# Attention sublayer: the output product done in two halves of the tokens, the first of them inside the attention steps

## The reference, cut to what matters

```
score = where(causal, sum_h relu(q_idx @ k_idx) * w_idx, -inf)      # per query token
sel   = top_k(score, 128)                                           # keys kept
logits= where(valid, q_lat @ c_sel * dh**-0.5, -inf);  p = softmax(logits)
o     = (p @ c_sel) @ w_uv                                          # 512 x 1024
x     = x + o.reshape(512, 1024) @ w_out                            # the output product
```

## Time and profile before

| | us |
|---|---|
| median of 3 runs (lowest, highest) | 2018.43 (2018.05, 2019.6) |
| the profiled execution itself | 2018.26 |
| its span, first to last instruction | 2016.4 |
| TensorE busy | 1980.2 |
| VectorE, ScalarE, GpSimd busy | 1346.0, 844.5, 249.7 |
| attention steps, turn_probs(0) to the first output matmul | 1554.35 to 1613.14 |
| output product | 1613.14 to 1656.80 |

### The profile page before, as it was taken

How to read it: one execution, slowest core, us unless ns; L and a number is a source line. 1 busy time by engine, 2 the same in 40 slices (tenths; PEclk the granted TensorE clock), 3 DMA queues, 4 the chain that set the end, 5 groups by cost and what they waited for, 6 DMA issues and landing times.

```text
span 2016.4 us, 23083 instructions
## 1 busy us (share of the span) xinstructions
PE 1980.2 (98%) x9030; PEld 1618.4 (80%) x9030; DVE 1346.0 (67%) x1673; ACT 844.5 (42%) x1151; POOL 249.7 (12%) x183
## 2 busy tenths in 40 slices
PE   8999999999999999999999999999998899999997
PEld 7788888877877888888888888888875688888886
DVE  7999944443534447999843899983458658999732
ACT  5555632132222224554631555562266535555520
POOL 0000012010010141000021000002224650000031
PEclk9999999999999999999999999999999999999998
DMA  4233123312212232242131333222231013322221
GB/s 168 84 122 129 58 102 112 113 64 100 84 68 85 82 105 84 84 147 104 58 115 64 119 141 110 84 87 100 81 105 42 1 63 142 109 84 98 100 93 65
DMA packets 69719, 189.45 MB, mean 94 GB/s; under 512 B 4016, under 2 KB 12208, under 8 KB 64496
## 3 DMA queue, kind: packets, MB, share of 16 engines
q1 hardware_dynamic: 69376, 187.25, 26.5%
q0 software_dynamic: 240, 0.79, 0.1%
HBM read 185.92 MB, written 2.10 MB: 93 GB/s over the span
## 4 chain that ended last, share of the span: by engine, by line
PE 87%; DVE 6%; issue 3%; ACT 2%; POOL 1%; SPq 0%; DMA 0%; POOLq 0%; DVEq 0%; ACTq 0%
PE bank L1804 13%; PE bank L1806 13%; PE bank L1805 13%; PE bank L1812 12%; PE bank L1814 12%; PE bank L1813 12%; PE bank L1818 2%; PE bank L1820 2%; PE bank L1819 2%; PE bank L2021 2%; PE bank L1911 2%; DVE part_lo L1182 1%; PE bank L2011 1%; PE bank L2130 1%; POOL dsa_temp L712 1%
## 5 line engine op out<-in xcount | busy, mean ns | idle before, releaser
L741 ACT ACTIVATE part_hi<-quad_w 128x1024 fp32r<-128x1024 f32 x280 | 293.2, 1064 | 279.5 <-PE bank L1814 199.8
L1182 DVE TENSOR_TENSOR part_lo<-quad_w,part_hi 128x1024 fp32r<-128x1024 f32 x280 | 330.0, 1217 | 25.7 <-ACT part_hi L741 25.3
L1804 PE MATMUL bank<-gated_hi,out_hi 128*128 128x512 f32 x704 | 274.8, 390 | 0.0
L1806 PE MATMUL bank<-gated_hi,out_lo 128*128 128x512 f32 x704 | 274.1, 389 | 0.0
L1805 PE MATMUL bank<-gated_lo,out_hi 128*128 128x512 f32 x704 | 274.1, 389 | 0.0
L1812 PE MATMUL bank<-part_hi,s_hi 128*128 128x512 f32 x640 | 252.6, 395 | 2.4 <-DVE part_lo L1182 2.4
L1814 PE MATMUL bank<-part_hi,s_lo 128*128 128x512 f32 x640 | 249.6, 390 | 0.0
L1813 PE MATMUL bank<-part_lo,s_hi 128*128 128x512 f32 x640 | 249.2, 389 | 0.0
L1812 PE MATMUL bank<-part_hi,xn_hi 128*128 128x512 f32 x608 | 238.8, 393 | 4.7 <-DVE part_lo L1182 4.7
L1814 PE MATMUL bank<-part_hi,xn_lo 128*128 128x512 f32 x608 | 237.9, 391 | 0.0
L1813 PE MATMUL bank<-part_lo,xn_hi 128*128 128x512 f32 x608 | 237.7, 391 | 0.0
(11 more groups left out here) (207 smaller groups left out, 3385.8 us busy)
## 6 DMA issues: line engine op xcount, KB each, us to landing
quad_w<-w_ffn_in SPq DMA_DIRECT2D x80, 1024.0 KB, 7.3
out_raw<-w_ffn_out SPq DMA_DIRECT2D x64, 704.0 KB, 4.0
w_raw<-w_ret_in SPq DMA_DIRECT2D x24, 1024.0 KB, 4.8
rest_raw<-w_ffn_in SPq DMA_DIRECT2D x32, 256.0 KB, 5.8
w_raw<-w_ret_out SPq DMA_DIRECT2D x8, 1024.0 KB, 4.8
w_raw<-w_dsa SPq DMA_DIRECT2D x8, 1024.0 KB, 4.8
x_res<-x_in SPq DMA_DIRECT2D x8, 256.0 KB, 6.3
out<-x_res SPq DMA_DIRECT2D x8, 256.0 KB, 2.2
```

The source lines that it names most:

```text
L741: nc.scalar.activation(in_four(part_hi[part_slot(h)]), source, copy).then_inc(part_hi_made, 1)
L1182: nc.vector.tensor_tensor(in_four(part_lo[part_slot(h)]), source, in_four(part_hi[part_slot(h)]).bitcast(FP32), ALU.subtract)\
L1804: mm(to, w_hi_of[:, at:at + width], hi, start=start, stop=False)
L1806: return mm(to, w_lo_of[:, at:at + width], hi, start=False, stop=stop)
```

## The change

The output product is done in two halves of 256 tokens. The first (blocks 0 and 1, "early") is done one tile a step at the head of steps 18 to 25, into bank 7, and VectorE adds each tile to `x_res` at the end of the same step of its list. The second ("late") follows the steps, into banks 0 and 1; its first two tiles begin with the heads 0 to 3. All four weight units are split before: units 8 and 9 get places of their own (where `xn_hi` and `xn_lo` lie), 10 and 11 go to the slots of `w_hi` and `w_lo`. ScalarE makes their hi at steps 2, 6 and 10 (before: unit 9 at step 8, 10 and 11 in the output product), GpSimd their lo: unit 9 before its step 8, unit 10 before step 12, unit 11 before step 16. Two rounds of the choice move from before step 0 into the steps, three steps have two rounds, and `result_hi` and `result_lo` come one step earlier. In the output phase the first four `stream_lo` wait until tile 3 is done.

```diff
--- before.py
+++ after.py
+    dsa_out_parts = [(at(f"dsa_out_hi{n}", x_at + (1 + n) * CHUNKS * chunk, UNIT, FP32R),
+                      at(f"dsa_out_lo{n}", x_at + (1 + n) * CHUNKS * chunk + 4 * UNIT, UNIT, FP32R))
+                     for n in range(2)]
...
-    ROUND_STEPS = (8, 10, 11, 13, 14, 16, 17, 18, 19, 20)
-    EARLY_ROUNDS = TOP_K // 8 - len(ROUND_STEPS)
-
-    POOL_SPLITS = (DSA_UNITS - DSA_OUT_UNITS - 2, DSA_UNITS - DSA_OUT_UNITS + 2)
+    ROUNDS_AT = {8: 1, 10: 1, 12: 1, 14: 1, 16: 1, 17: 1, 18: 2, 19: 2, 20: 2}
+    EARLY_ROUNDS = TOP_K // 8 - sum(ROUNDS_AT.values())
+    CHOICE_STEP = max(ROUNDS_AT) + 1
+    EARLY_OUT = 18
+    POOL_SPLITS = (DSA_UNITS - DSA_OUT_UNITS - 2, DSA_UNITS)
...
     def results_bank(q):
-        return bank[5 + q % 3]
+        return bank[5 + q % 2]
+    def early_out():
+        return bank[7][:, :HALF_SEQ]
+    def late_out(d):
+        return bank[d % 2][:, :HALF_SEQ]
...
                 split_unit(u0 + POOL_SPLITS[0] + 2)
+                split_unit(u0 + POOL_SPLITS[0] + 3)
                 for i in range(VECTOR_STEPS, len(STEPS)):
+                    if i == 2 * HEADS - 4:
+                        split_unit(u0 + POOL_SPLITS[0] + 4)
+                    elif i == 2 * HEADS:
+                        split_unit(u0 + POOL_SPLITS[0] + 5)
                     _, _, probs, _, _, at = step_bufs(i)
                     pool.wait_ge(inverted, i + 1)
                     nc.gpsimd.tensor_scalar(probs, probs, row_inv[:, at], None, ALU.mult)\
                         .then_inc(pool_probs_done, 1)
-                split_unit(u0 + POOL_SPLITS[0] + 3)
...
-            if n >= 2 and SUBLAYERS[stage_of(u)] != "ffn":
+            if SUBLAYERS[stage_of(u)] == "dsa" and n >= DSA_UNITS - DSA_OUT_UNITS:
+                act.wait_ge(unit_done, u - 3)
+            elif n >= 2 and SUBLAYERS[stage_of(u)] != "ffn":
                 act.wait_ge(unit_done, u - 1 + 2 * pair)
...
                 for i in range(len(STEPS)):
-                    if i == HEADS:
-                        split_unit(u0 + 9)
+                    if i in (2, 6, 10):
+                        split_unit(u0 + DSA_UNITS - DSA_OUT_UNITS + 1 + i // 4)
                     copy_probs_t(i)
                     if i + 2 < len(STEPS):
                         exps(i + 2)
-                    if i % 4 == 1 and i > 4:
+                    if i % 4 == 0 and i >= 4:
                         result_hi(i // 4 - 1)
                 result_hi(len(STEPS) // 4 - 1)
+                act.wait_ge(unit_done, u0 + DSA_UNITS - DSA_OUT_UNITS + 1)
                 for d in range(CHUNKS):
-                    if d % 2 == 1 and d // 2 + 2 < DSA_OUT_UNITS:
-                        split_unit(u0 + DSA_UNITS - DSA_OUT_UNITS + 2 + d // 2)
...
+                def early_update(d):
+                    dve.wait_ge(early_out_done, d + 1)
+                    to = cols(x_res, d)[:, :HALF_SEQ]
+                    nc.vector.tensor_tensor(to, early_out(), to, ALU.add).then_inc(early_updated, 1)
+                def late_update(d):
+                    to = cols(x_res, d)[:, HALF_SEQ:]
+                    nc.vector.tensor_tensor(to, late_out(d), to, ALU.add).then_inc(x_updated, 1)
                 for i in range(len(STEPS)):
                     invert(i)
                     if i + 2 < len(STEPS):
                         minimum(i + 2)
-                    if i in ROUND_STEPS:
+                    if i % 4 == 1 and i > 4:
+                        result_lo(i // 4 - 1)
+                    for n in range(ROUNDS_AT[i] if i in ROUNDS_AT else 0):
+                        if n > 0:
+                            mark_8(last_block)
                         find_8(last_block)
-                    elif i == ROUND_STEPS[-1] + 1:
+                    if i == CHOICE_STEP:
                         choice_to_bias(last_block)
-                    if i % 4 == 2 and i > 4:
-                        result_lo(i // 4 - 1)
+                    if 0 <= i - EARLY_OUT < CHUNKS:
+                        early_update(i - EARLY_OUT)
...
-                    update(s, d, 4 + d % 2, 1.0)
-                    if d % 2 == 1 and d // 2 + 2 < DSA_OUT_UNITS:
-                        split_unit(u + 2)
-                    stream_lo(s + 1, d)
+                    late_update(d)
+                    if d == 3:
+                        for e in range(4):
+                            stream_lo(s + 1, e)
+                    elif d > 3:
+                        stream_lo(s + 1, d)
...
+                def out_products(to, d, tokens, ks):
+                    u = u0 + DSA_UNITS - DSA_OUT_UNITS + d // 2
+                    pe.wait_ge(w_lo_made, u + 1)
+                    for k in ks:
+                        done = product(to, None, (d % 2 * HEADS + k) * P, cols(o_hi, k)[:, tokens],
+                                       cols(o_lo, k)[:, tokens], k == 0, k == HEADS - 1,
+                                       of=unit_bufs(u)[1:])
+                    return done
+                early, late = slice(0, HALF_SEQ), slice(HALF_SEQ, SEQ)
                 for i in range(len(STEPS)):
+                    d = i - EARLY_OUT
+                    if 0 <= d < CHUNKS:
+                        if d == 0:
+                            pe.wait_ge(o_lo_made, 4)
+                        else:
+                            pe.wait_ge(early_updated, d)
+                        out_products(early_out(), d, early, range(HEADS)).then_inc(early_out_done, 1)
                     turn_probs(i)
...
+                pe.wait_ge(o_lo_made, 7)
+                for d in range(2):
+                    out_products(late_out(d), d, late, range(HEADS // 2))
+                pe.wait_ge(o_lo_made, 8)
                 for d in range(CHUNKS):
...
+                    ks = range(HEADS // 2, HEADS) if d < 2 else range(HEADS)
+                    out_products(late_out(d), d, late, ks).then_inc(unit_done if d % 2 else half_done, 1)
```

More of the change, by code:

```diff
@@ L409, in unit_bufs @@
             return out_raw[n], out_hi[n], out_lo[n]
+        n = u - FIRST_UNIT[s] - (DSA_UNITS - DSA_OUT_UNITS)
+        if SUBLAYERS[s] == "dsa" and 0 <= n < 2:
+            return (w_raw[u % 2],) + dsa_out_parts[n]
         return w_raw[u % 2], w_hi[u % 2], w_lo[u % 2]
@@ L673, in split_unit @@
                     pool.wait_ge(w_lo_made, u)
-                    nc.gpsimd.tensor_tensor(w_lo[u % 2][:, :], w_raw[u % 2][:, :],
-                                            w_hi[u % 2][:, :].bitcast(FP32), ALU.subtract)\
+                    raw, hi, lo = unit_bufs(u)
+                    nc.gpsimd.tensor_tensor(lo[:, :], raw[:, :], hi[:, :].bitcast(FP32), ALU.subtract)\
                         .then_inc(w_lo_made, 1)
@@ L1744, in invert @@
                     nc.vector.reciprocal(row_inv[:, at], row_sum[:, at]).then_inc(inverted, 1)
-                    if i - 1 in ROUND_STEPS:
+                    if i - 1 in ROUNDS_AT:
                         mark_8(last_block)
@@ L2193, in results @@
                     pe.wait_ge(probs_t_copied, i + 1)
-                    if i % 4 == 0 and i >= 12:
-                        pe.wait_ge(o_lo_made, i // 4 - 2)
+                    if i % 4 == 0 and i >= 8:
+                        pe.wait_ge(o_lo_made, i // 4 - 1)
                     for j in range(b + 1):
@@ L2209, in _ @@
                 results(len(STEPS) - 1)
+                pe.wait_ge(o_lo_made, 7)
+                for d in range(2):
+                    out_products(late_out(d), d, late, range(HEADS // 2))
+                pe.wait_ge(o_lo_made, 8)
                 for d in range(CHUNKS):
-                    u = u0 + DSA_UNITS - DSA_OUT_UNITS + d // 2
-                    if d % 2 == 0:
-                        pe.wait_ge(w_lo_made, u + 1)
                     if d >= 2:
                         pe.wait_ge(x_updated, CHUNKS * s + d - 1)
-                    for k in range(HEADS):
-                        if d == 0:
-                            pe.wait_ge(o_lo_made, len(STEPS) // 4 - 1 + k // 4)
-                        done = product(bank[4 + d % 2][:, :], u % 2, (d % 2 * HEADS + k) * P,
-                                       cols(o_hi, k), cols(o_lo, k), k == 0, k == HEADS - 1)
-                    done.then_inc(unit_done if d % 2 else half_done, 1)
+                    ks = range(HEADS // 2, HEADS) if d < 2 else range(HEADS)
+                    out_products(late_out(d), d, late, ks).then_inc(unit_done if d % 2 else half_done, 1)
         final = ("norm", len(SUBLAYERS))
```

3 lines of the change are left out of this document (2 added, 1 removed).

## The result

The changed kernel takes 2033.57 us (median of 4 runs, 2033.13 to 2034.17) against 2018.24 of the kernel before: a ratio of 1.0073, interval 1.0059 to 1.0087. It is slower by 15.3 us, where 2033.0 was forecast. The profiled execution has a span of 2032.1 us, 15.7 more than before.

The account below looks back on a forecast made before the run. TensorE, busy 98% of the span, was taken as the bound, with some 13 us of waits to win. Terms: 9.8 + 22.0 - 0.4 - 20.6 + 3.0 + 1.0 = +14.8 on 2018.26, forecast 2033.0 us, range 2023 to 2039.

Parts of the forecast that it names:

- TensorE was to be idle for 6 us at turn_probs(4): Step 4: TensorE idle 6 us while VectorE's scaling takes about 4 us beside GpSimd's pass over unit 9.
- Start of the steps: Ahead of step 0: two rounds fewer, then ScalarE's table load is what comes late; -2.8 us.
- Units 9 and 10 through step 8: Steps 0 to 8: GpSimd's unit 9 pass stops VectorE's scaling, +4.9 us; ScalarE's unit 10 pass costs +1.5.
- GpSimd's passes ahead of scalings 12 and 16: Steps 12 and 16: units 10 and 11 each cost 4.60 less 0.85 idle time, 3.75 us; +7.4 after catching up.
- What goes between step 8 and the first early tile: Steps 8 to 18: 0.69 us waiting ahead of turn_probs(18) and unit 9's 0.5 behind step 8 go; -1.2 us.
- Clock: Half clock behind TensorE's idle stretches: one shrinks ahead of step 0, three new ones come; +1.0 us, ends -1 and +4.
- Early half: Steps 18 to 25: 192 matmuls add 23.0 us, product changes 0.5, idle time of 1.53 goes; net +22.0.
- Steps 26 to 31, late half and what lies behind it: After the early tiles: steps 26 to 31 -0.4 us, late half -20.6, late first weight part ahead of next sublayer +3.0.
- The extra cost of the two halves: Output product: 256 columns take more than half of 512, so both halves cost TensorE 2.4 us more than one product.
- A: Rival, steps 4 to 7: VectorE is not stopped by GpSimd's pass; 3.9 us less, 2029.2; chance 0.13.
- B: Rival, steps 12 and 16: GpSimd's passes half hidden; 3.7 to 5.5 less, 1 less at end, 2027.5; chance 0.13.
- C: Rival, whole change: faster if every split fits in its engine's idle time; -4.0 us, 2014.3; chance 0.11.

Follow-up runs that it names:

- experiment 6: On the changed kernel, units 9 to 11 split late: ScalarE behind steps 17, 19, 21, GpSimd ahead of scalings 19, 21, 23; 2017.28 us, ratio 0.9993.
- experiment 2: On the changed kernel, GpSimd's pass over unit 9's low part covers only 16 of 2048 columns; 2030.89 us, ratio 1.0060.
- Experiment 4: On the changed kernel, GpSimd's pass over unit 9 issued as 8 instructions of 256 columns, nothing left out; 2031.79 us, ratio 1.0064.
- experiment 3: On the changed kernel, GpSimd's passes over units 10 and 11 cover only 16 of 2048 columns each; 2023.77 us, ratio 1.0027.
- experiment 9: On the kernel before, only VectorE's rounds placed as in the changed kernel, no early tiles, no unit moved; 2019.71 us, ratio 1.0006.
- experiment 8: On the changed kernel, the edits of experiment 6 and experiment 7 together, nothing left out; 2013.79 us, ratio 0.9976.
- experiment 1: On the kernel before, the output product behind the steps done with each tile in two halves of 256 columns; 2021.34 us, ratio 1.0016.
- experiment 7: On the changed kernel, late half's VectorE work reordered: next sublayer's rest one tile earlier, stream_lo spread over tiles 3 to 7; 2030.60 us, ratio 1.0059.
- experiment 5: On the changed kernel, units 10 and 11 split later: ScalarE behind steps 19, 21, GpSimd ahead of scalings 21, 23; 2024.81 us, ratio 1.0028.
- experiment 10: Changed kernel, GpSimd's three passes ahead of scalings 19, 21, 23, ScalarE's unit 11 at step 21, units 9, 10 unmoved; 2020.51 us, ratio 1.0008.

## Why the prediction was right, and which terms were not

The forecast's mechanism held at the places that it named: the scaling of VectorE at 3.88 us once, waits of 4 us at turn_probs(12) and (16), no wait from the first early tile to turn_probs(26), a late part_lo. One sign was off: TensorE was to be idle for 6 us at turn_probs(4), and it was for 4.01, with another 0.89 just ahead, where it waited for ScalarE's copy. By terms:

- Start of the steps: -2.8 forecast, -2.95 measured. Right. Of the 4.05 us of idle time 1.28 are left, behind ScalarE's table load, which makes -2.77; the rest lies ahead of it.
- Units 9 and 10 through step 8: +4.9 and +1.5 forecast, 6.4 together. 6.21 measured (experiment 6 against the changed kernel), 4.05 of it GpSimd's pass and 2.16 ScalarE's two. Right. (Half clock is in it: from turn_probs(4) to (8) there are 6.25 us, and 5.79 in experiment 2, where the clock stays at 1.00.) The Trainium skill ("SBUF — State Buffer", on the port pair that VectorE and GpSimd share) has the two exclude each other for the whole instruction. Experiment 4 agrees with that: pieces of 0.70 us delay a scaling by at most 0.5, where the whole pass delayed it by 3.6.
- GpSimd's passes ahead of scalings 12 and 16: +7.4. The two waits shrank by 7.2 in experiment 3. Right.
- What goes between step 8 and the first early tile: -1.2 forecast. Experiment 6, with no pass left there, takes 16.96 us from turn_probs(8) to that tile for 18.40 before: -1.4. Right.
- Clock: +1.0 forecast, within ends of -1 and +4. This is the term that was too small. The granted clock went to 0.50 behind each of the three long stops, for 3.5 to 5.8 us of its work, and TensorE was the bound in part of each. At the first early tile experiment 3 has 9.9 less, and the waits make 7.2 of it: 2.7 us. With the half clock behind the late half, where sum_over_features comes 12.43 us after the sublayer's start for 10.88, 1.5 more come outside the steps. That is 4.2 us, against which stands what before lost behind its one stop: 0.9 by turn_probs(4) and 0.7 by turn_probs(8), as experiment 9 shows. So +1.0 should have been +3.3 to +3.5.
- Early half: +22.0 forecast, +20.6 measured (37.87 less 17.25). This term was too large. A tile takes 2.96 us, so 23.7 for the 23.5 that I had, but the steps' own work beside it takes 14.2 and not 15.72. I read this as follows, without a run made for it: busy time of matmuls counts each one's end, which lies under the next one's start where TensorE doesn't stop. What goes with the waits is therefore 3.1, and not the 1.53 that the windows show as idle.
- Steps 26 to 31, late half and what lies behind it: -0.4, -20.6 and +3.0, -18.0 together. Measured: 39.99 for 58.02, -18.0. One by one: steps 26 to 31 take 13.72 for 14.36, -0.6. The late tiles take 23.11 in experiment 8, where nothing stops them, -20.6. The changed kernel's 26.27 make the stop worth 3.2, of which 2.53 stand right ahead of the next sublayer. Right.

In sum, the steps to the first early tile were forecast at +9.8 and the clock's 1.0, and measured at +11.7 (1593.19 for 1581.53). The early half was 1.4 less than forecast, the next sublayer's clock 1.5 more: 11.7 + 20.6 - 18.0 + 1.5 = 15.8, for 14.8 forecast and 15.7 in the spans. The clock's error and the early half's have opposite signs, so that the forecast hit to half a microsecond owes something to chance; each of the other terms that a run measures was right to 0.3 us. The extra cost of the two halves, 2.4 in the forecast, is 2.7 by experiment 1.

Of the rivals, A fell by experiments 2 and 4 and B by experiment 3. C's price was nearly right: it forecast 4.0 us less than before if every split fits in idle time, and experiment 8 measured 4.9 less. But in experiment 6 every split fits, and it is only 1.4 less, which can't be told from no change: C's sum had no term for the stop at the end, which takes experiment 7's order to remove. It failed as a forecast of this change, since the splits stood where nothing covered them. The changed kernel's loss isn't in what it does, but in the order of three passes on two engines (16.5 us at the first early tile, experiment 6) and in VectorE's row at the end (3.0 us, experiment 7).

What stays open: why TensorE begins at full clock behind one stop of 2.53 us and at half clock behind others of the same length. Seven traces have this stop. In six of them the clock of the first 2 us behind it is 0.50 to 0.68 (the changed kernel and experiments 2, 4, 5, 6 and 10), in one, experiment 3, it is 1.00. Experiment 3 also multiplies other values in its output product, since it leaves part of two low parts unmade. Nothing here was run to tell the causes apart. The Trainium skill ("TensorE: Matmul & The Clock Gate", on the HAM clock gate) says that the monitor's window runs freely and doesn't start with the kernel, so that the same work meets it at another phase. The differing outcomes agree with that; no run shifted the stop on purpose.

## What to carry to other kernels

Work that is moved off the path must be put where its engine waits, and a light load over the span (GpSimd has 13%) says nothing of that: read the idle time ahead of the instructions between which it will stand, and ask which other engine it shuts out for as long as one of its instructions lasts. Where a filler makes the bound engine's step longer, it makes room on every other engine: move the auxiliary work into those steps, not ahead of them. And price a stop of the bound engine with the half clock that follows it, not only by its own length.
